# 80 products of the identity with itself on TensorE, ahead of the first sums of squares, in a one-core kernel of two transformer blocks

## What is computed

```
mod   = silu(c)     @ ada_w + ada_b      # shift, scale, gate for the latent tokens
mod_c = silu(c_ctx) @ ada_w + ada_b      # the same for the context tokens
hx = rmsnorm(x, norm_w)  * (1 + scale)   + shift
hc = rmsnorm(cx, norm_w) * (1 + scale_c) + shift_c
px = split_cols(hx @ w_in);  pc = split_cols(hc @ w_in)
# three attention mixers, gate, output projection, residual
```

## Time and profile before

| | |
|---|---|
| three runs | 2554.87, 2558.02, 2559.02 us; median 2558.02 |
| profiled execution | 2553.55 us, its span 2551.7 us |
| PE busy | 2443.0 us (96%), 14758 matmul records |
| PEld busy | 1986.0 us (78%) |
| DVE, ACT, POOL busy | 1346.9, 951.4, 541.7 us |
| mean granted TensorE clock | 0.99 of full speed |

### The profile page before, as it was taken

One profiled execution on the slowest core, in us unless ns is written; L12 is line 12 of the kernel. 1 busy time (PEld: TensorE's weight loads), 2 busy tenths in 40 slices (PEclk: granted clock), 3 DMA queues, 4 the chain that ended last, 5 costly groups with the idle time before them and its releaser, 6 DMA issues.

```text
span 2551.7 us, 38058 instructions
## 1 busy us (share of the span) xinstructions
PE 2443.0 (96%) x14758; PEld 1986.0 (78%) x14758; DVE 1346.9 (53%) x2731; ACT 951.4 (37%) x1751; POOL 541.7 (21%) x530
## 2 busy tenths in 40 slices
PE   6999999999998999999999999999999999999998
PEld 4777877878887778778778668888888767888887
DVE  4667756765417663666727745433335954433333
ACT  4364254452324542635245334222225333422222
POOL 2212222122343122221365232000003332100001
PEclk9999999999998999999999999999999999999999
DMA  7302422225124024132524111323323212223322
GB/s 276 138 2 74 174 64 71 84 81 190 56 79 165 26 104 177 39 133 83 195 91 136 59 56 60 109 83 114 97 80 99 75 50 71 87 84 106 99 82 76
DMA packets 66900, 250.36 MB, mean 98 GB/s; under 512 B 7969, under 2 KB 11553, under 8 KB 57377
## 3 DMA queue, kind: packets, MB, share of 16 engines
q1 hardware_dynamic: 62960, 236.36, 28.0%
q0 software_dynamic: 3248, 11.54, 1.4%
q10 hardware_dynamic: 512, 0.03, 0.0%
HBM read 243.67 MB, written 4.19 MB: 97 GB/s over the span
## 4 chain that ended last, share of the span: by engine, by line
PE 81%; DVE 8%; ACT 4%; issue 3%; POOL 2%; DVEq 1%; ACTq 0%; DMA 0%; SPq 0%; POOLq 0%
PE ps L2542 34%; PE ps L2371 20%; PE ps L569 5%; PE ps L597 5%; PE ps L637 4%; PE ps L2519 4%; DVE ps L1951 2%; ACT probs L786 2%; PE ps L2352 1%; PE ps L2255 1%; POOL split_panels_first L1048 1%; PE ps L2390 1%; PE ps L2485 1%; PE ps L2559 1%; PE ps L2300 0%
## 5 line engine op out<-in xcount | busy, mean ns | idle before, releaser
L2542 PE MATMUL ps<-h_split,split_panels 128*128 128x512 f32 x2928 | 685.7, 393 | 1.8 <-ACT projected L1497 0.8
L2542 PEld LDWEIGHTS ps<-h_split,split_panels 128*128 128x128 f32 x2928 | 545.9, 188 | 126.8 <-issue 13.7
L2371 PE MATMUL ps<-h_split_first,split_panels_first 128*128 128x512 f32 x2808 | 555.6, 356 | 8.7 <-DVE h_split_first L1819 5.1
L2371 PEld LDWEIGHTS ps<-h_split_first,split_panels_first 128*128 128x128 f32 x2808 | 454.9, 191 | 84.0 <-DVE h_split_first L1819 6.8
L1048 POOL TENSOR_TENSOR split_panels_first<-panels_first,split_panels_first 128x1024 fp32r<-128x1024 f32 (+1 forms) x104 | 233.4, 2245 | 567.6 <-ACT split_panels_first L1238 567.6
L1896 DVE TENSOR_TENSOR split_panels<-panels,split_panels 128x1024 fp32r<-128x1024 f32 (+2 forms) x171 | 192.6, 1126 | 297.9 <-ACT split_panels L1246 294.1
L1246 ACT ACTIVATE split_panels<-panels 128x1024 fp32r<-128x1024 f32 (+2 forms) x210 | 204.3, 974 | 344.9 <-PE ps L2542 343.6
L1731 DVE SCALAR_TENSOR_TENSOR ps<-modulation_panels,silu_c,ps 128x256 f32<-128x256 f32 x480 | 225.3, 487 | 30.4 <-issue 2.1
L2542 PE MATMUL ps<-ffn_hidden_split,split_panels 128*128 128x512 f32 x990 | 225.1, 389 | 0.0
L2542 PEld LDWEIGHTS ps<-ffn_hidden_split,split_panels 128*128 128x128 f32 x990 | 185.9, 188 | 38.5
L1059 POOL TENSOR_TENSOR probs_turned<-probs_turned,probs 128x512 f32<-128x512 f32 x30 | 41.8, 1392 | 769.8 <-ACT probs L1440 769.8
(11 more groups left out here) (300 smaller groups left out, 2928.2 us busy)
## 6 DMA issues: line engine op xcount, KB each, us to landing
modulation_panels<-in_ada SPq DMA_DIRECT2D x64, 1024.0 KB, 5.0
panels<-in_w SPq DMA_DIRECT2D x88, 512.0 KB, 3.6
panels_first<-in_in SPq DMA_DIRECT2D x72, 512.0 KB, 5.9
panels<-in_in SPq DMA_DIRECT2D x42, 512.0 KB, 3.6
panels_first<-in_out SPq DMA_DIRECT2D x32, 384.0 KB, 3.1
panels<-in_w SPq DMA_DIRECT2D x32, 384.0 KB, 3.1
panels<-in_w SPq DMA_DIRECT2D x32, 320.0 KB, 2.9
panels<-in_out SPq DMA_DIRECT2D x16, 512.0 KB, 3.6
```

The costliest lines, as they stand in the source:

```text
L2371: ins = mm(at0, split1[:, s, w, c, :], hs1[:, h, c, lo:e], start=c == 0 and i == 0, stop=c == KC - 1 and i == 2)
L2542: ins = mm(out, split[:, n % SPLIT, a, c - base, :], moving(b, c), start=first and i == 0 and j == 0, stop=last and i == len(chunks) - 1 a ...
```

## The change

A constant says how often, and behind the wait for the matrices TensorE multiplies the identity by itself that many times into the first 128 columns of bank 0, each product for itself, with no signal. Nothing reads them. All lines behind the constant move down by two, and those behind the loop by four.

```diff
@@ -69,6 +69,8 @@
 KEYS = 4
+
+WARM_UP = 80
@@ -2355,6 +2357,8 @@
             both = [(0, SEQ), (SEQ, CTX)]
             pe.wait_ge(mats_in, 16)
+            for _ in range(WARM_UP):
+                mm(bank(0, 0, P), ident, ident, start=True, stop=True)
             sum_squares(0, TOK // P)
             pe.wait_ge(silu_done, 3)
             mod_rows_of(0)
```

## The result

With 80 products the kernel takes 2562.07 us in the median of 11 runs (2560.12 to 2565.38), before 2558.02 us (11 runs, 2554.2 to 2559.36): **+4.05 us**, a ratio of 1.0018 with a 95% interval of 1.001 to 1.0026. The forecast was +4.7 and 2562.7 us. The direction is clear of noise; the size (+2.6 to +6.7 us by the interval) can't be told from the 0.2% (5.1 us) at which the prediction drew its border.

What follows compares the result with a forecast made beforehand. It took TensorE, busy 96% of the span, to bound the kernel. A start 8.8 us later, less 4.6 given back, plus 0.5 for a clock fall, gave +4.7: 2562.7 us, range 2557 to 2568.

Steps and rivals of the forecast that it cites:

- Start and length of the products: At the kernel's start: 160 records from about 4.3 us, 20.6 us long, so the sums of squares start 8.8 us later.
- ends of 3.4 and 7.3: Low and high end for how many us TensorE's low clock lasts under the products; 5 us was taken.
- The gain behind them: Work from the sums of squares to the turning's end runs at full clock: 4.6 us given back.
- The fall under the sums: The clock may fall again under the one-column sums of squares: cost 0 to 1.6 us, 0.5 taken.
- the 6.8 us of the sum at full clock: Forecast time at 2.4 GHz for sums of squares, first modulation rows, roots and turning together, instead of 11.43 us.
- The signs that the prediction named: Profile readings at the start to confirm it: products' pitch and end, sums 2.5 us, turning's end about 32, projection 36.5 to 37.
- hidden delay: Rival at the start: transfers run at their limit until 45 us and absorb the later start; 2553.4 to 2558 us, chance 12%.
- slowness by transfers: Rival at the start: transfers, not the clock, slow the early records, so nothing is given back; 2564.5 us, chance 4%.
- a clock that stays low: Rival at the start: clock stays low under the products, which last 34.1 us; about +20, 2578 us, chance 5%.
- The faster one: Rival at the start: products at 0.061 us a record end at 15.8, ahead of 16.06; -6.2, 2551.8 us, chance 5%.
- What hides behind what: Up to the first projection: ScalarE's copy fits with 0.5 us to spare; GpSimd's splits, until 33.4, stay covered.
- the same addition holds for both times: Whole kernel: +4.7 us added to the profiled execution (2553.55 to 2558.3) and to the median (2558.02 to 2562.7).

Runs made afterwards that it cites:

- e2: 160 products instead of the change's 80: 2581.81 us, +22.6 against the kernel before, ratio 1.009.
- e5: 46 products instead of the change's 80: 2556.39 us, -1.25 against the kernel before, ratio 0.9994.
- e6: 46 products at the start, plus 10 in TensorE's gap ahead of the first projection: 2554.47 us, -3.17 against the kernel before, ratio 0.9983.
- e10: Repeat of e6, 46 products and 10 in the gap: 2554.82 us, -3.25 against the kernel before, ratio 0.9986.
- e1: 40 products instead of the change's 80: 2555.66 us, -3.55 against the kernel before, ratio 0.9989.
- e7: 20 products instead of the change's 80: 2559.46 us, +1.82 against the kernel before, ratio 1.0002.
- e3: The change's 80 products, but of the identity with one column of ones: 2581.16 us, +21.95 against the kernel before, ratio 1.0086.
- e4: No products; TensorE waits ahead of the sums until GpSimd has cleared an unused tile seven times: 2561.10 us, +1.89 against the kernel before, ratio 1.001.
- e8: No products, otherwise the changed kernel's code, a single run: 2558.25 us.

## Why the prediction was right, step by step

- **Start and length of the products.** Forecast: 4.3 us, 20.6 us long with 5 us at the low level, end 24.9. The profile: 4.50, 20.86 us, end 25.36, with 6.2 us at the low level, inside the ends of 3.4 and 7.3. Two records for each product, 0.213 and 0.114 us: right. The sums start 9.3 us later (8.8 forecast, ends 8.0 and 9.8). That the 5 us fitted is partly luck: the pitch changed 2.8 us behind the first product in e2, below the low end, 4 to 4.5 in e5, e6 and e10, and 5.6 to 6 in e1 and e7. The high end of 7.3 counts from the start of the transposes; the granted clock itself was low for 6.9 us there.
- **The gain behind them.** Forecast: 4.6 us if the clock stays up. From the start of the sums to the end of the turning it is 33.92 - 25.36 = 8.56 us instead of 11.43, a gain of 2.9. What is missing is the fall of the clock.
- **The fall under the sums, the step that was mis-sized.** I had booked 0.5 us between the ends 0 and 1.6. Against the 6.8 us of the sum at full clock the profile has 8.56, so it cost 1.7. All six profiles whose sums began at full clock behind wide products show a fall between the start of the sums and the roots (with 80, at 27.7; e1, e2, e5, e6, e10), where I had booked it at a third of its price. In e1, e6 and e10 the low stretch lasted 6.8 us. What sets the fall off is not shown: in four of the six it came during the sums, in e2 only under the modulation rows (45.1 us) and in e5 behind the pause for a panel, and no run put other work in the place of the sums.
- **A gain that I had not booked.** Behind the gap of 2.2 us ahead of the first projection the clock did not fall in the changed kernel: 12 records in 2.35 us (38.58 on) instead of 3.92. It did fall there in e1, e2, e3, e4, e5, e7 and e8, behind gaps of 2.4 to 2.8 us; whether the shorter gap or chance made the difference is not shown. So the delay is 6.4 us where the turning ends (33.92 against 27.49) and 4.9 at the projection's end (40.93 against 36.07). The 4.7 of the forecast meets this 4.9 by luck: the later start (+0.5) and the fall (+1.2) against the gain that was not booked (-1.6). Such a stretch is there in one execution and not in another, so the median need not be what one profile shows.
- **The signs that the prediction named.** Met: the start, pitch and end of the products, and transposes that start later by more than 4 us (130.64 against 123.90). Missed: sums in 2.5 us (2.95), the end of the turning at about 32 (33.92), the first projection at 36.5 to 37 (38.58), and no pause other than the one ahead of the projection (there is one of 0.58 us). The fall of the clock and the start that came 0.5 us late account for the missed times; the projection's own full clock then makes up for them.
- **Nothing hides the delay.** Right: at the end of the first projection e2 is 22.9 and e3 22.7 us behind the kernel before, and their medians are 22.6 and 21.95 higher. The rivals of hidden delay and of slowness by transfers have fallen (e2; e3), and that of a clock that stays low is what one-column products give, not these. The faster one has fallen too: the products behind the change of pitch took 0.11 us a record and ended at 25.36, far behind 16.06.
- **What hides behind what.** Mostly right. One wait is new: the second pair of modulation rows waits 0.58 us for GpSimd's split of a panel (until 34.48). The split is over at 34.38 us, 7.1 us later than before where 6.1 were reckoned, because the sums end 7.1 us later. I had looked only at the projection as a user of the split, and missed that these rows stand behind the same wait. It costs nothing, since the normalised chunk comes later still.
- **Profile and median.** The profiled execution lies 4.5 us below its median before and 0.8 above it after, so their difference of 9.3 is more than twice the change's. I had said that the same addition holds for both times, which stands for the kernel and not for a single pair of executions. The profiles show where the rest comes from (TensorE's timeline of the changed kernel, then stretches: us, PE, granted clock, DMA share, GB/s, of the changed kernel, of e8, which has no products, and of the kernel before):

```profile
130.64 2.82 PE L599 MATMUL ps<-matrices,probs 128*128 128x128 f32 x12 [3.00 <-ACT probs L788]
...
142.48 0.27 PE L613 MATMUL ps<-matrices,wide_weights 128*128 128x128 f32 x1
```
```profile
230.00:232.00 2.00, 2.00 (x10) 0.50 0.00 0
225.00:227.00 2.00, 2.00 (x11) 0.50 0.00 0
219.00:235.00 16.00, 13.99 (x95) 1.00 0.07 14
```

  The changed kernel is 4.9 us behind at the projection's end, 6.7 at 130.64, 5.5 at 142.48 (137.03 before) and 9.3 at the end. Low stretches lie in it that the profile before lacks, and this one lies in e8 too, as does another (at 346 us with 80 products, at 341 in e8, a granted clock of 1.00 there before), so these are not the products' doing. The profile before has a mean granted clock of 0.990, which 5 of 69 further runs of that kernel reached.

What stays open: the time of e4, whose interval is too wide, the source of e1's gain, what sets off the fall of the clock behind the products, and the squares' delay in the profiles with products.

## What to carry to other kernels

Products that only keep TensorE's clock up paid here as far as they fitted into time in which it waited anyway. Reckon their length from the pitch of the same records at both levels, let them end when the awaited data comes, and count every one beyond that at its full price: here 40 products gained 3.6 us, 46 gained 1.3 (not clear of nothing), 80 lost 4, 160 lost 23, and 20, which ended 5 us early, gained nothing. Then look at the work behind them, whether the clock holds under it, and try a few more in the next idle gap: 46 and ten together gained 3.2 us in two sets of runs, by estimate half of it from the ten.

## What the runs showed of the hardware that I had not expected

- Products of one column did not raise the clock: 34 us of them without a pause left it at 1.2 GHz by their pitch (e3). The clock fell during the sums (2.7 to 3.7 us of such products) or during the modulation rows behind them in each of the six profiles in which 12 to 37 us of wide products had gone before.
- The spread of the runs goes with the clock. Of 69 runs of the kernel before in the three sets, the 7 with a mean granted clock of 0.985 took 2562.5 us on average, the 35 with 0.988 took 2557.9, and the 5 with 0.990 took 2554.8. So equal programs differ by 8 us, twice what the change itself costs, and the difference goes with the share of time at the low level.
- The granted clock reads 1.00 from the start of a record up to its first fall, while the pitch of the records (0.213 us) is the one that they have at a granted 0.50 (e7). For the first microseconds of a kernel the pitch is the measure.
